# Products of a constant tile in TensorE's waits at five norms, in the pool layer and at the end of attention

## The chip, the cores and the metric

The kernel runs on one core of one Trainium2 chip. The metric is the device time of one execution in microseconds (us). The engines are TensorE (PE; its weight loads are shown as PEld), VectorE (DVE), ScalarE (ACT), GpSimd (POOL) and SyncE (SP), whose queue issues the weight transfers.
## What is computed

Two transformer blocks over 256 tokens of width 1024. The first block has one mixer made of three (an RWKV-7 recurrence, a sparse attention, an S5 state space), a convolutional FFN and a gated embedding ("ple"). The second block is two layers: a causal pooling mixer with an FFN, then dilated attention in three branches with an FFN. Cut to what matters here:

```
# first block, after its mixer
x = x + rms_norm(conv_ffn(rms_norm(x, pre_ffn_norm)), post_ffn_norm)   # FFN 0, norm 3 = post_ffn
x = x + rms_norm(p @ w_ple, ple_norm) * gate(x @ w_ple_gate)           # "pg" and "pl"
# second block
for layer in range(2):
    h = modulate(rmsnorm(x, norm1[layer]), sh1, sc1)      # norm 5 (layer 0), norm 7 (layer 1)
    if layer == 0: y = pool_mixer(h, w_in, w_grp, scale, w_out)
    else:
        kv = modulate(rmsnorm(x, kv_norm), ...) @ w_kv    # from the same x as norm 7
        y = dilated_attention(h, kv, w_q, w_o)
    x = x + g1 * y
    h = modulate(rmsnorm(x, norm2[layer]), sh2, sc2)      # norm 6 (layer 0), norm 8 (layer 1)
    x = x + g2 * conv_ffn(h, w_up, conv, w_down)          # FFN 1, FFN 2 (width 2816)
return rmsnorm(x, final_g)                                # norm 9
```

## The kernel before

Activations lie transposed: 8 tiles of 128 channels by 256 tokens. The program is written by hand, one instruction stream for each engine, with semaphores between them; TensorE executes its stream in order. Weights are streamed by SP as chunks of 1 MB into a ring of six slots. To reach the needed precision each fp32 operand is split in a high and a low part: ACT rounds a chunk to `ring_hi` (four slots), POOL subtracts it to give `ring_lo`, and TensorE does three products for each pair of tiles (high by high, high by low, low by high), accumulated in one of eight PSUM banks. A chunk gives two output tiles of 8 k-steps by 3 products, 48 products of 128x256.

Every dense stage follows an RMS norm of its input, and the norm is a chain that crosses the engines: TensorE sums the squares with `ones_mean` as one-column products (`mean_square_of`, called at the end of `ffn` and `last_tile`), ACT and DVE form the reciprocal root (`rs`), TensorE spreads it over a bank with four products by `ident` (`spread`, after it has waited on `rs_small`), DVE scales h by it, and ACT and DVE split the result, tile by tile, into `hn_hi` and `hn_lo`. TensorE begins the next stage in `first_tiles`: it opens three or four banks, waits for the chunks, and then for each k waits on `x_high` (the k-th high part is there) and does two products for each of the banks; the low parts come after, with `x_split`. The rest of the stage are `split_tile` calls, which wait for nothing but banks and chunks.

`opened(job)` takes the next bank in turn and waits until its last user is done; `held_back` and `gathered` take one out of the turn for a sum; `close` signals a finished job on `psum_ready`, in the order in which jobs were numbered.

The order of the work around the change is: `ple(3)`, `ffn(0, ...)` with norm 3 at its end, `projection(2, "pg", ...)` with norm 5 at its end (through `last_tile`), the pool layer (`first_tiles(3, ...)`, `grouped` and `pooled` by turns, the last of which is `pooled(3)` with its tiles 6 and 7), `projection(4, "po", ...)` with norm 6, `ffn(1, ...)` with norm 7, keys, values and attention, `dil_values(15)`, the output projection with norm 8, and `ffn(2, ...)` with norm 9. POOL writes the constants (`ident`, `ones_mean`, masks) at the start.

Of the kernel before, what the change touches and what calls it, by code (L numbers as in the profile page):

```python
# [10 lines left out]
F32 = mybir.dt.float32  # L11
# [5 lines left out]
P = 128  # L17
# [56 lines left out]
def two_block_kernel(nc, a, out):  # L74
    ctx = ExitStack()
    with ctx:
        sems = {}

        def sem(name):
            if name not in sems:  # L80
                sems[name] = ctx.enter_context(nc.semaphore(name))
            return sems[name]

        def sb(name, cols, rows=P):
            return ctx.enter_context(nc.sbuf_tensor(name, [rows, cols], F32))
# [4 lines left out]

        ident = sb("ident", P)
        ones_mean = sb("ones_mean", P)
        head_ones = sb("head_ones", P)
        head_mean = sb("head_mean", P)
# [369 lines left out]
        def _(pe):  # L465
# [29 lines left out]
            def opened(job):  # L495
                bank = next_bank()
                numbered(job, bank)
                return banks[:, bank, :]
# [23 lines left out]
            def chunk(key):  # L522

                if key not in begun:
                    in_turn(key)
                    begun.add(key)
                    if key == early[0]:
                        pe.wait_ge(sem("early_hi"), 1)
                    elif key in early:
                        pe.wait_ge(sem("early_lo"), early.index(key))  # L530
                    elif key in split:
                        pe.wait_ge(sem("lo_ready"), split_no[key] + 1)
                    else:
                        pe.wait_ge(*chunk_landed[key])
                used_at[key] = job_no[current[0]]
                chunk_used[key] = (psum_ready, used_at[key] + 1)
                if key in split or key in early:
                    k, n = KT if key in early else chunk_src[key][0].shape[1], 0
                    n = chunk_flat(key)[0].shape[1] // k
                    return [shaped(part, k, n) for part in chunk_flat(key)[1:]]  # L540
                return chunk_view(key)
# [8 lines left out]
            def close(ins, jobs=1):  # L550
                ins.then_inc(psum_ready, jobs)
# [44 lines left out]
                                            k == 0, k == KT - 1)  # L596
                close(last)

            def first_tiles(rnd, jobs, x, ks=tuple(range(KT)), ms=None, norm=None):

                low, high = x
                todo = []
                if norm is not None:
                    b_ms = opened(("ms", norm[0]))
                for job, key, c0 in jobs:
                    b = opened(job)[:, 0:T]
                    todo.append((b, [v[:, :, c0:c0 + P] for v in chunk(key)]))
                for n, k in enumerate(ks):
                    pe.wait_ge(sem("x_high"), KT * (rnd + 1) + n + 1)
                    for b, (w_lo, w_hi) in todo:  # L610
                        mm(b, w_hi[:, k, :], high[:, k, :], start=(n == 0), stop=False)
                        mm(b, w_lo[:, k, :], high[:, k, :], start=False, stop=False)
                for t, (b, (_, w_hi)) in enumerate(todo):
                    for n, k in enumerate(ks):
                        if t == 0:
                            pe.wait_ge(sem("x_split"), KT * (rnd + 1) + n + 1)
                        if t == 0 and n == KT - 1 and norm is not None:
                            mean_square_of(norm[0], b_ms, norm[1], (0,))
                        if t == len(todo) - 1 and n == KT - 1 and ms is not None:
                            gathered(ms)  # L620
                        last = mm(b, w_hi[:, k, :], low[:, k, :], start=False, stop=(n == KT - 1))
                    close(last, 2 if ms is not None and t == len(todo) - 1 else 1)

            def mean_square_of(i, b, sq, ks):

                for k in ks:
                    if i == 2:
                        pe.wait_ge(sem("squares_summed"), 1)
                    elif i in SUMMED and k == 0:
                        copied(("acc", i))  # L630
                    elif i in SUMMED:
                        pe.wait_ge(sem("squares"), square_base[i] + k + 1)
                    elif k % 2 == 0 or k == KT - 1:
                        pe.wait_ge(sem("squares"), square_base[i] + (1, 1, 2, 2, 3, 3, 4, 5)[k])
                    for s in range(2):
                        last = mm(b[:, s:s + 1], sq[:, k, s * P:s * P + P], ones_mean[:, 0:1],
                                  start=(k == s == 0), stop=(k == KT - 1 or i == 2), skip_group_check=True)
                if ks[-1] == KT - 1 or i == 2:
                    close(last)
                    if i in SUMMED:  # L640
                        held.remove(bank_no["acc", i])

            def spread(i, scratch=True):
                for x in range(3 if scratch else 0):
                    opened(("xs", i, x))
                b = opened(("wd", i))
                pe.wait_ge(sem("rs_small"), NORM_ORDER.index(i) + 1)
                for s in range(2):
                    last = mm(b[:, s * P:s * P + P], rs_of(i)[:, 2 + s:3 + s].broadcast_to([P, P]), ident[:, :])
                close(last, 4 if scratch else 1)  # L650

            def projection(rnd, name, key, x, ms=None, ks=tuple(range(KT))):

                tiles = [((name, m), (key, m // 2), 128 * (m % 2)) for m in range(8)]
                first_tiles(rnd, tiles[:4], x, ks, ms[0] if ms else None)
                for t in tiles[4:7]:
                    split_tile(*t, x)
                if ms is None:
                    split_tile(*tiles[7], x)
                    return  # L660
                last_tile(tiles[7][0], tiles[7][1], x, ms)

            def last_tile(job, key, x, ms):

                b = opened(job)
                current_job = current[0]
                b_ms = opened(("ms", ms[0]))
                current[0] = current_job
                w = chunk(key)
                for k in range(KT):  # L670
                    last = three_passes(b[:, 0:T], [v[:, k, 128:256] for v in w], [v[:, k, :] for v in x],
                                        k == 0, k == KT - 1)
                close(last)
                mean_square_of(ms[0], b_ms, ms[1], (0, 6, 7))
                if ms[0] != 1:
                    spread(ms[0])
# [488 lines left out]
            def ffn(f, first, ms):  # L1165
                tiles = [((nm, f, 2 * i + x), (nm, f, i), 128 * x) for i in range(FT // 2) for nm in ("ug", "uu")
                         for x in range(2)]
                begin = 4 if f else 3
                first_tiles(first, tiles[:begin], (hn_lo, hn_hi), norm=None if f else (2, sqb))
                if f == 0:  # L1170
                    for bank in kept:
                        held.remove(bank)
# [59 lines left out]
                            close(last_turn(s, k))  # L1232

            ple(3)
            ffn(0, 1, (3, sqb))
            projection(2, "pg", "pleg", (hn_lo, hn_hi), (5, sqb))

            def grouped(gq):
                for i in range(2):
# [7 lines left out]
                    close(last)  # L1247

            def pooled(gq):
                for s in range(2):  # L1250
                    copied(("pv", gq, s))
                for m in (2 * gq, 2 * gq + 1):
                    b = opened(("pp", m))
                    mm(b[:, 0:BAND0], pv[:, 0, m * P:m * P + P], bands[:, gq, 0:BAND0], stop=False, skip_group_check=True)
                    close(mm(b[:, P:T], pv[:, 1, m * P:m * P + P], bands[:, gq, BAND0:BAND0 + P], start=False,
                             skip_group_check=True))

            tiles = [(("pi", m), ("pin", m // 2), 128 * (m % 2)) for m in range(8)]
            first_tiles(3, tiles[:4], (hn_lo, hn_hi))
            split_tile(*tiles[4], (hn_lo, hn_hi))  # L1260
            pe.wait_ge(sem("bands_ready"), 1)
            grouped(0)
# [72 lines left out]
            def dil_values(i):  # L1335
# [18 lines left out]
                for x in range(2):  # L1354
# [2 lines left out]
                close(last)  # L1357

            first_tiles(6, [(("dk", 0, br, i), ("kv", 4 * br), 128 * i) for br in range(2) for i in range(2)],
                        (hn_lo, hn_hi))  # L1360
            for i in range(2):
                keys(0, 2, i)
            for br in range(3):
# [28 lines left out]
            for i in range(16):  # L1392
# [11 lines left out]
                if i >= 13:  # L1404
                    out_begun(2)
            dil_values(15)
            pe.wait_ge(sem("x_high"), KT * 10)
            pe.wait_ge(sem("x_split"), KT * 10)
            gathered(8)
            for m, bank in enumerate(out_banks):  # L1410
                numbered(("dw", m), bank)
                held.remove(bank)
# [66 lines left out]
        def _(pool):  # L1479
# [14 lines left out]
                keep_if(v, ALU.is_ge, size - 1, -1, neg)  # L1494

            led.emit(g.memset(ident[:, :], 0.0), sem("ident_ready"))
            keep_if(ident[:, :], ALU.not_equal, 0, 1, [[-1, P]], 1.0, sem("ident_ready"))
            led.emit(g.memset(ones_mean[:, :], 1.0 / D))
            led.emit(g.memset(head_ones[:, :], 1.0))
# [1469 lines left out]
```

## Time and profile before

| | |
|---|---|
| time, median of 3 runs | 1344.93 us (1342.05 to 1350.05) |
| span of the profiled execution | 1340.4 us |
| mean granted clock over the span | 0.974 |
| PEld, DVE, ACT, POOL busy | 89%, 42%, 46%, 63% |
| DMA | 242.82 MB, mean 181 GB/s |

The profiled execution is given by its span, from the first to the last instruction; no time of its own is given beside it. The runs' times are of other executions. The page has the busy time of each engine, the span in 40 slices, the chain of work that ended last, and the costliest groups of instructions. The granted clock of a stretch shows whether TensorE ran at its high level in it.

### The profile page before, as it was taken

What the parts mean: (1) busy time and instruction counts of PE and PEld (TensorE: products, weight loads), DVE (VectorE), ACT (ScalarE), POOL (GpSimd) and SP (SyncE); (2) the same over time, 40 slices, a digit from 0 to 9 for tenths busy, and PEclk for the clock granted to TensorE, in tenths of its full rate; (3) what the DMA queues carried; (4) which work ended last, traced back from release to release, by engine and by line L of the source; (5) the groups of instructions that cost most, each with busy time, mean ns of one, the idle gap of its engine ahead of it and who ended that gap; (6) DMA issues with size and microseconds to landing.
All of it is one profiled execution on the core that took longest, in us unless ns stands there. A gap on an engine that the chain in (4) does not pass through costs nothing.

```text
span 1340.4 us, 25785 instructions
## 1 busy us (share of the span) xinstructions
PE 1278.5 (95%) x10737; PEld 1192.8 (89%) x10737; DVE 564.4 (42%) x1275; ACT 621.8 (46%) x962; POOL 849.0 (63%) x441
## 2 busy tenths in 40 slices
PE   7998989889999999899999999999999998999998
PEld 6984548679999999899999999999998888999998
DVE  5658686633666653513333203132222224433301
ACT  5531443136655644653544434554534454544442
POOL 7985400027798696564887786856745665788772
PEclk9998999989999999898999999999999999999999
DMA  8749995504455555334555554453648793455550
GB/s 266 205 158 371 345 334 206 189 1 158 145 177 183 173 174 188 126 122 162 165 182 189 173 174 157 145 165 98 191 127 263 233 291 123 139 181 188 174 173 32
DMA packets 232817, 242.82 MB, mean 181 GB/s; under 512 B 9068, under 2 KB 201726, under 8 KB 232702
## 3 DMA queue, kind: packets, MB, share of 16 engines
q1 hardware_dynamic: 232382, 241.08, 55.3%
q8 instruction: 86, 1.41, 0.4%
q14 instruction: 29, 0.24, 0.1%
q10 hardware_dynamic: 320, 0.10, 0.0%
HBM read 240.11 MB, written 1.05 MB: 180 GB/s over the span
## 4 chain that ended last, share of the span: by engine, by line
PE 83%; DVE 4%; ACT 2%; issue 1%; DVEq 0%; ACTq 0%
PE banks L548 81%; PE banks L1332 1%; DVE arena L1693 1%; DVE arena L1686 1%; ACT arena L2432 1%; DVE banks L1686 0%; DVE banks L1693 0%; ACT ring_hi L2432 0%; DVE arena L1699 0%; ACT hn_hi L2432 0%; PE banks L558 0%; PE banks L861 0%; PE banks L984 0%; ACT L2432 0%; DVE arena L1690 0%
## 5 line engine op out<-in xcount | busy, mean ns | idle before, releaser
L1613 POOL TENSOR_TENSOR ring_lo<-ring,ring_hi 128x2048 fp32r<-128x2048 f32 (+1 forms) x176 | 719.0, 4096 | 423.5 <-ACT ring_hi L2432 423.4
L548 PE MATMUL banks<-hn_hi,ring_lo 128*128 128x256 f32 (+1 forms) x1864 | 525.4, 287 | 0.0
L548 PE MATMUL banks<-hn_hi,ring_hi 128*128 128x256 f32 x1696 | 484.0, 289 | 11.8 <-ACT hn_hi L2432 11.0
L548 PE MATMUL banks<-hn_lo,ring_hi 128*128 128x256 f32 x1696 | 445.8, 283 | 0.0
L2432 ACT ACTIVATE ring_hi<-ring 128x2048 fp32r<-128x2048 f32 (+1 forms) x176 | 299.6, 1704 | 171.2 <-PE banks L548 127.3
L548 PEld LDWEIGHTS banks<-hn_hi,ring_lo 128*128 128x128 f32 (+1 forms) x1864 | 363.6, 196 | 0.1
L548 PEld LDWEIGHTS banks<-hn_hi,ring_hi 128*128 128x128 f32 x1696 | 333.1, 196 | 15.2 <-issue 9.4
L548 PEld LDWEIGHTS banks<-hn_lo,ring_hi 128*128 128x128 f32 x1696 | 310.5, 192 | 0.1
L2432 ACT ACTIVATE arena<-banks 128x256 f32<-128x256 f32 (+6 forms) x238 | 92.4, 409 | 242.7 <-PE banks L548 173.0
L548 PEld LDWEIGHTS banks<-arena 64*128 64x128 f32 (+4 forms) x1282 | 115.4, 178 | 62.2 <-issue 38.9
L548 PE MATMUL banks<-arena 128*64 128x128 f32 (+9 forms) x1282 | 143.1, 305 | 21.2 <-DVE arena L1686 8.7
L548 PE MATMUL banks<-act_hi,ring_hi 128*128 128x256 f32 x528 | 149.7, 283 | 0.0
L548 PE MATMUL banks<-act_hi,ring_lo 128*128 128x256 f32 x528 | 149.4, 283 | 0.0
L548 PE MATMUL banks<-act_lo,ring_hi 128*128 128x256 f32 x528 | 149.4, 283 | 0.0
L1693 DVE SCALAR_TENSOR_TENSOR arena<-banks,par,arena 128x255 f32<-128x255 f32 (+1 forms) x187 | 89.6, 481 | 121.3 <-ACT arena L2432 118.8
L2432 ACT ACTIVATE arena<-banks,par 128x256 f32<-128x256 f32 x88 | 49.7, 565 | 123.0 <-PE banks L548 70.8
L548 PEld LDWEIGHTS banks<-act_lo,ring_hi 128*128 128x128 f32 x528 | 101.4, 192 | 0.0
L548 PEld LDWEIGHTS banks<-act_hi,ring_lo 128*128 128x128 f32 x528 | 101.4, 192 | 0.0
L548 PEld LDWEIGHTS banks<-act_hi,ring_hi 128*128 128x128 f32 x528 | 101.4, 192 | 0.0
L1693 DVE SCALAR_TENSOR_TENSOR h<-banks,mod,h 128x256 f32<-128x256 f32 x32 | 15.5, 484 | 134.8 <-PE banks L548 134.8
L2432 ACT ACTIVATE arena<-arena 128x256 f32<-128x256 f32 (+4 forms) x97 | 46.9, 512 | 36.5 <-DVE arena L1922 12.7
L548 PE MATMUL banks<-ring_lo,hn_hi 128*128 128x256 f32 x208 | 58.9, 283 | 0.0
(263 smaller groups left out, 1579.5 us busy)
## 6 DMA issues: line engine op xcount, KB each, us to landing
ring<-in_ada_w_dram SPq DMA_DIRECT2D x48, 1024.0 KB, 8.9
ring<-in_ffn_w_up_dram SPq DMA_DIRECT2D x44, 1024.0 KB, 5.2
ring<-in_w_up_dram SPq DMA_DIRECT2D x22, 1024.0 KB, 5.1
ring<-in_ffn_w_down_dram SPq DMA_DIRECT2D x16, 1024.0 KB, 4.9
ring<-in_w_kv_dram SPq DMA_DIRECT2D x15, 1024.0 KB, 5.5
ring<-in_w_in_dram SPq DMA_DIRECT2D x9, 1024.0 KB, 8.4
ring<-in_w_kv_dram SPq DMA_DIRECT2D x18, 512.0 KB, 4.0
ring<-in_attn_w_q_dram SPq DMA_DIRECT2D x18, 512.0 KB, 3.9
```

The costliest lines, as they stand in the source:

```text
L548: return nc.tensor.matmul(o, l, r, start=start, stop=stop, **k)
L1332: last = nc.tensor.transpose(b[:, br * P:br * P + P], dsc[s][:, x, k * P:k * P + P], ident[:, :])
L1613: led.emit(g.tensor_tensor(low, raw, high.bitcast(F32), ALU.subtract), sem("lo_ready"))
L1686: led.emit(v.tensor_tensor(o, x, y, op), signal, value)
L1693: led.emit(v.scalar_tensor_tensor(out=o, in0=x, scalar=s, in1=y, op0=op0, op1=op1), signal, value)
L2432: led.emit(nc.scalar.activation(o, x, func, **k), signal, value)
```

## The change

A constant tile `steady` of 128x128 ones (fp32r) is written by POOL at the start. A helper `steadied(o, n)` issues n products of it with itself, read as 256 columns, into a bank that the next job has opened and not yet begun; the job's first product starts the bank anew, so that what stood there is dropped. 112 such products are issued, each group ahead of one of TensorE's waits:

- in `spread`, 5 each at norms 3, 5, 6, 7 and 8, before the wait on `rs_small`;
- in `last_tile` at norm 5, 16 before the sums of squares;
- in `first_tiles` before the first wait on `x_high`: 13 at `projection(2, ...)`, 9 at the pool layer, 8 each at `ffn(1, ...)`, `ffn(2, ...)` and the keys;
- in `pooled`, 12 at tile 6; the bank is now opened before the wait for the copies (`copied(("pv", ...))`), in all four calls;
- after `dil_values(15)`, 13; `gathered(8)` is moved ahead of the waits on `x_high` and `x_split`.

TensorE's stream has in addition one wait on `steady_ready` after `ple(3)`.

```
+        steady = ctx.enter_context(nc.sbuf_tensor("steady", [P, P], F32R))
...
+            def steadied(o, n):
+                for _ in range(n):
+                    mm(o[:, 0:T], steady[:, :], steady[:, :].unsqueeze(1).broadcast_to([P, 2, P]))
...
-            def first_tiles(rnd, jobs, x, ks=tuple(range(KT)), ms=None, norm=None):
+            def first_tiles(rnd, jobs, x, ks=tuple(range(KT)), ms=None, norm=None, idle=0):
...
+                steadied(todo[0][0], idle)
                 for n, k in enumerate(ks):
                     pe.wait_ge(sem("x_high"), KT * (rnd + 1) + n + 1)
...
                 b = opened(("wd", i))
+                if i in (3, 5, 6, 7, 8):
+                    steadied(b, 5)
                 pe.wait_ge(sem("rs_small"), NORM_ORDER.index(i) + 1)
...
-            def projection(rnd, name, key, x, ms=None, ks=tuple(range(KT))):
+            def projection(rnd, name, key, x, ms=None, ks=tuple(range(KT)), idle=0):
...
-                first_tiles(rnd, tiles[:4], x, ks, ms[0] if ms else None)
+                first_tiles(rnd, tiles[:4], x, ks, ms[0] if ms else None, idle=idle)
...
                 close(last)
+                if ms[0] == 5:
+                    steadied(b_ms, 16)
                 mean_square_of(ms[0], b_ms, ms[1], (0, 6, 7))
...
-                first_tiles(first, tiles[:begin], (hn_lo, hn_hi), norm=None if f else (2, sqb))
+                first_tiles(first, tiles[:begin], (hn_lo, hn_hi), norm=None if f else (2, sqb), idle=8 if f else 0)
...
             ple(3)
+            pe.wait_ge(sem("steady_ready"), 1)
             ffn(0, 1, (3, sqb))
-            projection(2, "pg", "pleg", (hn_lo, hn_hi), (5, sqb))
+            projection(2, "pg", "pleg", (hn_lo, hn_hi), (5, sqb), idle=13)
...
             def pooled(gq):
-                for s in range(2):
-                    copied(("pv", gq, s))
                 for m in (2 * gq, 2 * gq + 1):
                     b = opened(("pp", m))
+                    if m == 6:
+                        steadied(b, 12)
+                    if m == 2 * gq:
+                        for s in range(2):
+                            copied(("pv", gq, s))
...
-            first_tiles(3, tiles[:4], (hn_lo, hn_hi))
+            first_tiles(3, tiles[:4], (hn_lo, hn_hi), idle=9)
...
-                        (hn_lo, hn_hi))
+                        (hn_lo, hn_hi), idle=8)
...
             dil_values(15)
+            gathered(8)
+            steadied(bank_of(("acc", 8)), 13)
             pe.wait_ge(sem("x_high"), KT * 10)
             pe.wait_ge(sem("x_split"), KT * 10)
-            gathered(8)
...
             led.emit(g.memset(ident[:, :], 0.0), sem("ident_ready"))
+            led.emit(g.memset(steady[:, :].bitcast(F32), 1.0), sem("steady_ready"))
```

## Rows read from the trace of the kernel before

**Rows 1.** The page: busy time, and the chain that ended last by engine.
```profile
PE 1278.5 (95%) x10737; PEld 1192.8 (89%) x10737; DVE 564.4 (42%) x1275; ACT 621.8 (46%) x962; POOL 849.0 (63%) x441
...
PE 83%; DVE 4%; ACT 2%; issue 1%; DVEq 0%; ACTq 0%
```

**Rows 2.** TensorE's waits by releaser: us in total, times, longest.
```profile
PE banks L548 <- ACT hn_hi L2432: 12.2, 13, 1.8
...
PE banks L548 <- DVE rs L1699: 4.1, 6, 0.8
```

**Rows 3.** Busy time by stretch; after the engines the granted clock, DMA share, GB/s.
```profile
530.46:537.29 6.83, 5.44 (x25) 5.47 (x26) 6.65 (x19) 3.72 (x12) 0.00 (x0) 0.50 0.22 75
561.18:568.01 6.83, 4.88 (x22) 4.58 (x22) 4.79 (x12) 3.09 (x9) 0.00 (x0) 0.50 0.10 30
602.14:605.55 3.41, 3.41 (x18) 3.41 (x18) 0.85 (x2) 1.17 (x4) 0.97 (x1) 0.50 1.10 360
629.45:636.28 6.83, 5.65 (x28) 5.55 (x27) 6.49 (x16) 3.95 (x9) 1.95 (x1) 0.50 0.26 87
827.42:830.83 3.41, 3.11 (x14) 3.14 (x15) 3.30 (x9) 2.09 (x6) 0.00 (x0) 0.50 0.15 50
1138.03:1144.86 6.83, 6.13 (x29) 6.16 (x30) 6.38 (x16) 4.56 (x9) 4.22 (x1) 0.50 0.25 79
```

**Rows 4.** TensorE in order of time around norm 3: start, us, instruction, idle before.
```profile
527.31 1.40 PE L548 MATMUL banks<-ones_mean,arena 128*128 128x1 f32 x12
529.35 0.68 PE L548 MATMUL banks<-ident,rs 128*128 128x128 f32 x4 [0.65 <-DVE rs L1699]
531.85 0.55 PE L548 MATMUL banks<-hn_hi,ring_hi 128*128 128x256 f32 x1 [1.81 <-ACT hn_hi L2432]
...
532.41 0.41 PE L548 MATMUL banks<-hn_hi,ring_hi 128*128 128x256 f32 x1
532.62 0.41 PE L548 MATMUL banks<-hn_hi,ring_lo 128*128 128x256 f32 x1
```

**Rows 5.** The chain that ended last, in order of time: FFN 1's products.
```profile
630.76 192.74 PE banks L548 x1584
```

**Rows 6.** ACT in order of time: last high parts after norms 3 and 6.
```profile
538.71 0.38 ACT L2432 ACTIVATE hn_hi<-banks 128x256 fp32r<-128x256 f32 x1
...
635.48 0.47 ACT L2432 ACTIVATE hn_hi<-banks,mod 128x256 fp32r<-128x256 f32 x1 [0.44 <-DVE banks L1693]
```

**Rows 7.** TensorE in order of time around norm 5.
```profile
559.74 1.50 PE L548 MATMUL banks<-ones_mean,arena 128*128 128x1 f32 x12 [2.24 <-DVE arena L1686]
562.01 1.19 PE L548 MATMUL banks<-ident,rs 128*128 128x128 f32 x4 [0.77 <-DVE rs L1699]
564.39 0.55 PE L548 MATMUL banks<-hn_hi,ring_hi 128*128 128x256 f32 x1 [1.18 <-ACT hn_hi L2432]
```

**Rows 8.** TensorE in order of time at the pool layer's last tiles.
```profile
600.83 1.17 PE L548 MATMUL banks<-late,arena 128*128 128x144 f32 x8 [1.88 <-ACT arena L2432]
```

**Rows 9.** TensorE in order of time around norm 7.
```profile
825.86 0.68 PE L548 MATMUL banks<-ident,rs 128*128 128x128 f32 x4 [0.74 <-DVE rs L1699]
827.72 0.55 PE L548 MATMUL banks<-hn_hi,ring_hi 128*128 128x256 f32 x1 [1.18 <-ACT hn_hi L2432]
```

**Rows 10.** TensorE in order of time at attention's end.
```profile
1124.06 0.36 PE L548 MATMUL banks<-hn_hi,ring_hi 128*128 128x256 f32 x1 [1.83 <-ACT hn_hi L2432]
```

**Rows 11.** Busy time by stretch: before norm 6's fall, and at attention's end.
```profile
626.03:629.45 3.42, 2.44 (x21) 2.23 (x19) 0.65 (x2) 0.68 (x2) 3.42 (x2) 1.00 0.45 137
...
1120.97:1124.38 3.41, 1.58 (x27) 1.36 (x24) 1.34 (x4) 1.00 (x2) 0.00 (x0) 1.00 0.01 2
```

**Rows 12.** POOL in order of time at the start.
```profile
1.46 0.20 POOL L1498 MEMSET ones_mean<- 128x128 f32 x1
...
12.25 4.55 POOL L1517 TENSOR_TENSOR ring_lo<-ring,early_hi 128x2048 fp32r<-128x2048 f32 x1 [0.45 <-ACT early_hi L2432]
```

**Rows 13.** The page's costliest group: POOL's low parts of the weights.
```profile
L1613 POOL TENSOR_TENSOR ring_lo<-ring,ring_hi 128x2048 fp32r<-128x2048 f32 (+1 forms) x176 | 719.0, 4096 | 423.5 <-ACT ring_hi L2432 423.4
```

## Prediction, made before the change was run

> **What bounds the kernel now.** I read the page first: TensorE is busy for 95% of the span and is 83% of the chain that ended last [rows 1]. A change gains only if TensorE's own work gets shorter or its waits do. Next its waits by releaser: the two steps of a norm that it waits for, the spread of the reciprocal root and the first high part, cost 4.1 and 12.2 us in all [rows 2]. The change shortens no such wait: what TensorE waits for is made by ACT and DVE. So I looked at the clock. In stretches around the norms the granted clock is 0.50, the 1.2 GHz level. Six of them lie at the places of the change, 34.1 us together: after norms 3, 5, 6, 7 and 8, and at the pool layer's end [rows 3]. Each begins inside or just after a wait, and for most of it TensorE has products to do; the order of time shows what they cost there: two products of 256 columns start 0.21 us apart (532.41, 532.62) [rows 4], and the same form runs at 192.74 / 1584 = 0.122 us in FFN 1, nearly all of it at 1.00 [rows 5]. That is what can be won: 0.213 less 0.122, or 43% of each slow stretch in which TensorE is bound by its own products. The 16 us of waits stay.
>
> **The change part by part.**
>
> *What the slow stretches cost.* At each place: the time from the first dense product to the end of the stretch, times 0.43.
> - Norm 3: 531.85 to 537.29 is 5.44 us, so 2.3 us. But here the high parts come slowly. The last begins at 538.71 and takes 0.38 [rows 6], and the products that wait for it would begin at about 539.2 and end at 540.2. As it is, 25 slow ones of the 64 are done by 537.29 and the other 39 end at 537.29 + 39 x 0.122 = 542.0. So the gain is 1.8 us.
> - Norm 5: 564.39 to 568.01 is 3.62 us, so 1.55. The four spreading products are slow too, 1.19 us [rows 7] for 0.68 at norm 7 [rows 9]: 0.5 more. Together 2.05.
> - Pool's end: the stretch of 3.41 us is full of products [rows 3]: 1.45.
> - Norm 6: 630.76 [rows 5] to 636.28 is 5.52 us: 2.35. The last high part is done at 635.95 [rows 6]; TensorE at full clock needs it at 630.76 + 56 x 0.122 = 637.6. It stays the bound, and the same holds for norms 5, 7 and 8, whose high parts follow the same steps.
> - Norm 7: 827.72 [rows 9] to 830.83 is 3.11 us: 1.35.
> - Norm 8: its wait is that of norm 7. The slow stretch has 6.13 us of TensorE's work in it, dense products [rows 3]: 2.6.
>
> The sum is 1.8 + 2.05 + 1.45 + 2.35 + 1.35 + 2.6 = 11.6 us.
>
> *Do the added products hold the clock?* No row before has a filler. What the rows show is which kind of work goes with a fall. Ahead of the fall at norm 6 TensorE is recorded busy for 2.44 of 3.42 us, and yet the clock falls [rows 11]; most of these records are one-column products such as those of rows 4, which last 0.12 us each and stream nothing. At attention's end the busy time is only 1.58 of 3.41 us, most of it wider products of attention's values, and the clock stays [rows 11]. So the recorded busy time alone does not tell; the kind of product matters, and the fillers are 256 columns wide. Bounds for the effect: 0 (they do nothing) and all of the 11.6. I take all of it, for the reason that they have the form of the stream in which the clock is 1.00.
> The Trainium skill, "TensorE: Matmul & The Clock Gate", Part 4 (PE-mode transpose), says that transposes do not count as busy for the gate in the way other products do. By that rule a kind that does not count would bring none of the 11.6; the fillers are plain products, but whether ones multiplied with ones count is what no row shows.
>
> *What the fillers cost.* One costs 0.122 us at the high level, 0.213 at the low one. They run in waits whose end ACT or DVE sets, so only what sticks out counts. Waits and fillers (at 0.122): norm 3, 0.65 for 5 (0.61) and 1.81 for 13 (1.59) [rows 4]; norm 5, 2.24 for 16 (1.95), 0.77 for 5 (0.61), 1.18 for 9 (1.10) [rows 7]; pool's end 1.88 for 12 (1.46) [rows 8]; norms 6, 7, 8 each 0.74 for 5 (0.61) and 1.18 for 8 (0.98) [rows 9], of which the other two are like it; attention's end 1.83 for 13 (1.59) [rows 10]. In all 112 fillers, 13.7 us, in 16.1 us of waits. Each fits, two with under 0.1 us to spare; I put 0.3 us for those, bounds 0 and 1. Behind the fillers on TensorE stand the spread and the first products, for which the whole next stage waits, so anything that sticks out is paid in full. At the low level the same 112 last 23.9 us, 7.8 more than the waits: that is the price if the cover is gone.
>
> *The moved steps.* In `pooled` the bank is opened before the wait for the copies; both waits were passed before the same product, so the later one still sets it: 0. The bank of tile 6 was last that of tile 3, long split. `gathered(8)` takes the bank of a transpose whose copies `dil_values(15)` had already waited for: 0. The wait on `steady_ready` is for something 500 us old.
>
> *The memset.* POOL gets one more 128x128 memset, 0.20 us by the one of the same size; POOL then waits 0.45 us for ACT before the first low part [rows 12]. Hidden; without that wait 0.2.
>
> *What is late next.* TensorE reaches each stage's later chunks up to 2.6 us sooner. POOL makes a chunk's low part in 4.1 us [rows 13], TensorE uses it up in 48 x 0.122 = 5.9 us, and during each norm the ring fills. So I expect no new wait for weights. If there were one at each stage, it could take back what was won: bounds 0 and 11.6, and I take 0.
>
> So this execution would be 11.6 - 0.3 = 11.3 us shorter: 1329.1 for its span of 1340.4. The median of the runs shown stands 4.5 us above that span; a time of the profiled execution itself is not given. All six places lost the clock in it, which an average execution need not do, and at two the stretch was half as long as elsewhere; I take 85% of the gain for the median: 9.6 us, **1335.3 us**. The Trainium skill, same page, Part 1, says that the number of slow products at a start changes from run to run of one kernel. That is no term of the sum; the rows of one execution can't show it.
>
> **The rivals.**
>
> *A. Ones do not count.* The clock falls as before and the fillers behind a fall run slow. For it: nothing in the trace shows such a product holding the clock. Against it: the form. Price by the starts of the slow stretches [rows 3]: at norm 3 the 13 fillers begin at 530.03, 4 run fast and 9 slow, 2.4 us in 1.81, 0.6 over; norm 5, 5 and 9 slow, 0.3 and 0.75 over; norm 6, 8 slow, 0.5 over; norm 8 0.15. Together 2.3: 1347.2 us.
>
> *B. The gain is won and given back.* The clock holds, but the next stage waits for weights or, as at norm 3, for the split of the activations. For it: at norm 3 the high parts are the bound as soon as the clock holds, and at the pool layer's end the DMA is at 360 GB/s in the slow stretch [rows 3]. Against it: POOL's 4.1 us a chunk. If half comes back, 11.3 / 2: about 5 us gained, 1340 us. A case that falls short of the whole for another cause, such as fewer falls in the runs, ends there too.
>
> *C. Slower: the fillers stick out.* One mechanism: they run at 0.213 us or more, because the clock is already low at each wait or each of them loads `steady` afresh without overlap. All 112 then cost 7.8 us over the waits and nothing is won: 1352.7 us. It is slower beyond what can be told only if a filler costs on average over (16.1 + 6.7) / 112 = 0.20 us, with no gain beside it. Against it: every product in the stream loads its own weights and takes 0.122.
>
> **How the numbers follow.** About 0.5%, 6.7 us, is what a measurement of this kernel can tell from no change. The forecast case gets 0.68, A 0.12, B 0.14, C 0.06. Of the forecast case (own range 1329 to 1339) a tenth gives under 6.7 us. Faster 0.62, same 0.32, slower 0.06. The range goes from 1329 (the whole 11.3 and a saving in variance between executions) to 1344, which takes in B and leaves most of A and C out.
>
> **What would show it.** Right: in the profile after, the six stretches of 0.50 are gone, the mean granted clock is about 0.99 (34.1 us at half are 0.013 of the span), the fillers last 0.12 us each, the first dense product of each stage starts at the same distance from the last sum of squares as before, and its successors are 0.12 apart. The stretches of 0.50 before 300 us and the one at the end stay. Wrong: a clock of 0.50 behind fillers (A), idle time before `ring_lo` or `hn_hi` products in the 10 us after a norm (B), or a spread that starts later after the squares than 0.74 us (C).

## The result and the profile after

The changed kernel takes 1337.23 us (median of 6 runs, 1330.9 to 1340.5), the kernel before 1346.61 us in as many (1342.05 to 1350.05). The ratio is 0.9924, 95% interval 0.9899 to 0.9949: 10.2 us less. The profiled execution has a span of 1329.0 us and a mean granted clock of 0.984; before it was 1340.4 and 0.974.

The page after, first busy time, then the chain. They are nearly those of [rows 1]: the busy time of TensorE has not gone down, since fillers took the place of slow products.

```profile
PE 1279.6 (96%) x10849; PEld 1194.0 (90%) x10849; DVE 564.3 (42%) x1275; ACT 621.1 (47%) x962; POOL 849.6 (64%) x442
...
PE 82%; DVE 4%; ACT 2%; issue 1%; POOL 1%; DMA 1%; DVEq 0%; ACTq 0%
```

Busy time by stretch, after, with the columns of [rows 3]: the 7 us behind norms 3, 6, 7, 8 and the pool layer, and the one slow stretch that is left of the 34.1 us, at norm 5. It is the second row, with 0.50.

```profile
528.72:535.55 6.83, 6.66 (x52) 6.09 (x51) 6.65 (x18) 3.29 (x10) 0.00 (x0) 1.00 0.28 98
559.92:563.33 3.41, 3.41 (x19) 3.41 (x18) 3.34 (x8) 2.06 (x5) 0.00 (x0) 0.50 0.00 0
...
597.00:604.00 7.00, 6.94 (x58) 6.97 (x59) 0.85 (x2) 1.75 (x5) 2.35 (x1) 1.00 0.85 285
624.30:631.10 6.80, 6.66 (x56) 6.46 (x55) 6.62 (x16) 4.09 (x9) 1.89 (x1) 1.00 0.22 74
818.70:825.50 6.80, 6.66 (x55) 6.46 (x55) 6.61 (x16) 4.08 (x9) 0.00 (x0) 1.00 0.23 78
1128.60:1135.40 6.80, 6.28 (x53) 6.31 (x53) 6.58 (x16) 4.05 (x9) 4.84 (x2) 1.00 0.30 97
```

The 52 products in the first row are not to be compared with the 25 of [rows 3] as they stand, since the fillers in front of the first dense product are among them. Counted from the first dense product of the stage, 25 dense products start in 5.44 us before (531.85 to 537.29) and 40 after (530.44 to 535.88).

TensorE in order of time after, around norm 3, 6 and 7: start, us, instruction, idle before. The fillers end about when the wait does, and the dense products, from the second on, start 0.12 us apart instead of 0.21.

```profile
526.99 0.47 PE L549 MATMUL banks<-ones_mean,arena 128*128 128x1 f32 x3
527.32 0.84 PE L549 MATMUL banks<-steady 128*128 128x256 f32 x5
528.01 0.71 PE L549 MATMUL banks<-ident,rs 128*128 128x128 f32 x4
528.48 1.79 PE L549 MATMUL banks<-steady 128*128 128x256 f32 x13
530.44 0.38 PE L549 MATMUL banks<-hn_hi,ring_hi 128*128 128x256 f32 x1 [0.17 <-ACT hn_hi L2449]
530.66 0.28 PE L549 MATMUL banks<-hn_hi,ring_lo 128*128 128x256 f32 x1
530.78 0.28 PE L549 MATMUL banks<-hn_hi,ring_hi 128*128 128x256 f32 x1
...
623.55 0.71 PE L549 MATMUL banks<-ident,rs 128*128 128x128 f32 x4
...
817.97 0.71 PE L549 MATMUL banks<-ident,rs 128*128 128x128 f32 x4
```

The same view around norm 5, where the clock fell at 559.92: the 9 fillers behind the spread run slowly and last 1.99 us, and with them the first dense products.

```profile
554.54 2.07 PE L549 MATMUL banks<-steady 128*128 128x256 f32 x16
556.94 1.50 PE L549 MATMUL banks<-ones_mean,arena 128*128 128x1 f32 x12 [0.33 <-DVE arena L1703]
558.30 0.84 PE L549 MATMUL banks<-steady 128*128 128x256 f32 x5
559.12 0.71 PE L549 MATMUL banks<-ident,rs 128*128 128x128 f32 x4
559.58 1.99 PE L549 MATMUL banks<-steady 128*128 128x256 f32 x9
561.37 0.42 PE L549 MATMUL banks<-hn_hi,ring_hi 128*128 128x256 f32 x1
561.59 0.41 PE L549 MATMUL banks<-hn_hi,ring_lo 128*128 128x256 f32 x1
```

And at norm 8: the 8 fillers of FFN 2 begin 0.52 us late, because they stand behind the wait for a weight chunk.

```profile
1127.89 0.71 PE L549 MATMUL banks<-ident,rs 128*128 128x128 f32 x4
1129.12 1.18 PE L549 MATMUL banks<-steady 128*128 128x256 f32 x8 [0.52 <-POOL ring_lo L1630]
1130.14 0.28 PE L549 MATMUL banks<-hn_hi,ring_hi 128*128 128x256 f32 x1
```

### The profile page after: what moved, and what is told of

The parts are those of the page before. It is cut to its first block, busy times and chain, and to the rows that moved or that the text cites. A ratio compares the mean times of both kernels' runs of the same rounds, so it can differ in the third digit from the quotient of the medians.

```text
span 1329.0 us, 26012 instructions
## 1 busy us (share of the span) xinstructions
PE 1279.6 (96%) x10849; PEld 1194.0 (90%) x10849; DVE 564.3 (42%) x1275; ACT 621.1 (47%) x962; POOL 849.6 (64%) x442
## 4 chain that ended last, share of the span: by engine, by line
PE 82%; DVE 4%; ACT 2%; issue 1%; POOL 1%; DMA 1%; DVEq 0%; ACTq 0%
PE banks L549 79%; PE banks L1347 1%; POOL ring_lo L1630 1%; DVE arena L1710 1%; DVE arena L1703 1%; ACT ring_hi L2449 1%; ACT arena L2449 1%; DMA ring<-in_w_kv_dram 1%; DVE banks L1703 0%; DVE arena L1716 0%; DVE banks L1710 0%; PE banks L559 0%; PE banks L872 0%; PE banks L995 0%; ACT hn_hi L2449 0%
## 5 line engine op out<-in xcount | busy, mean ns | idle before, releaser
L549 PE MATMUL banks<-hn_hi,ring_lo 128*128 128x256 f32 (+1 forms) x1864 | 517.6, 284 | 0.0
L549 PE MATMUL banks<-hn_hi,ring_hi 128*128 128x256 f32 x1696 | 476.1, 286 | 4.0 <-ACT hn_hi L2449 2.8
L549 PEld LDWEIGHTS banks<-hn_hi,ring_lo 128*128 128x128 f32 (+1 forms) x1864 | 356.8, 192 | 0.1
L549 PEld LDWEIGHTS banks<-hn_hi,ring_hi 128*128 128x128 f32 x1696 | 326.3, 192 | 7.8 <-ACT hn_hi L2449 4.4
```

Of the source, the lines that this page charges most:

```text
L549: return nc.tensor.matmul(o, l, r, start=start, stop=stop, **k)
```

## The experiments

Each was timed in five rounds against the kernel before, on the same chip, with 6 to 12 executions of its own. The ratio is that to before. "Slow from 500 us" is the sum of the stretches at 0.50 in the profiled execution from 500 us to the start of its last norm. "Slow in all" is worked out for each execution from its mean granted clock c and its span, (1 - c) x 2 x span, and averaged over the executions.

```
kernel             ratio   95% interval      slow from 500 us   slow in all   times from .. to
before                                        34.1               83.2          1341.8 .. 1350.8
the change         0.9924  0.9899 .. 0.9949    3.4               49.4          1330.9 .. 1340.5
e1_moves           1.0006  0.9984 .. 1.0028   34.1               82.1          1341.0 .. 1354.1
e2_narrow          1.0017  0.9998 .. 1.0035   34.1               87.1          1343.0 .. 1354.0
e3_zeros           0.9909  0.9880 .. 0.9939    6.8               48.9          1330.6 .. 1341.7
e4_double          0.9975  0.9955 .. 0.9996    0.0               54.2          1337.7 .. 1348.5
e5_transposes      0.9927  0.9902 .. 0.9952    3.4               49.2          1330.3 .. 1342.0
e6_early           0.9891  0.9866 .. 0.9915    0.0               27.9          1328.7 .. 1330.0
e7_half            0.9949  0.9926 .. 0.9973   10.2               58.4          1332.6 .. 1345.4
e8_no_first        0.9955  0.9932 .. 0.9977   13.7               58.8          1332.1 .. 1342.9
e9_early_only      0.9968  0.9950 .. 0.9986   34.1               60.1          1339.7 .. 1346.5
e10_behind_chunks  0.9882  0.9854 .. 0.9910    0.0               29.2          1330.0 .. 1333.4
```

The row of before is of the 29 executions that e1 to e4 were timed against. The 28 that e5 to e8 were timed against have 77.0 us slow in all, and the 17 of e9 and e10 have 82.3; so differences of a few us in that column say nothing.

**The moved steps without the products.**

```
             def steadied(o, n):
-                for _ in range(n):
-                    mm(o[:, 0:T], steady[:, :], ...)
+                return
```

> The change without its 112 products: the constant tile, its memset, the wait on it, the bank opened ahead of the copies in the pool layer and the sum's bank taken ahead of the waits at attention's end are all kept. Theory (the gain is the held clock): time as before, ratio 1.000 within its interval, and slow stretches (granted clock 0.50) at most or all of the six places, some 25 to 34 us of them from 500 us on. Rival (the moved steps or the shifted addresses bring the gain): the ratio stays at 0.992, about 10 us less than before.

Measured: 1.0006, all six stretches back. Busy time by stretch of this kernel, two of the six:

```profile
530.37:537.20 6.83, 5.40 (x25) 5.43 (x26) 6.65 (x19) 3.68 (x12) 0.00 (x0) 0.50 0.22 77
...
1137.94:1144.77 6.83, 5.88 (x27) 5.91 (x28) 6.63 (x16) 4.31 (x9) 4.48 (x1) 0.50 0.28 91
```

The moved steps, the memset and the shifted addresses do nothing that can be measured; the products bring the gain.

**The same number of products, 2 columns wide.**

```
-                    mm(o[:, 0:T], steady[:, :], steady[:, :].unsqueeze(1).broadcast_to([P, 2, P]))
+                    mm(o[:, 0:2], steady[:, :], steady[:, 0:2])
```

> The same 112 products at the same places, but each streams 2 columns where the change streams 256; the weight load of 128x128 is the same. Theory (what counts is the kind of product, and the gain is the held clock): the clock falls at most of the six places as before, and the ratio is 0.998 to 1.001. Rival 1 (keeping TensorE occupied or primed brings the gain, whatever it streams): ratio 0.992 to 0.994 and no fall. If each costs as much as a sum-of-squares product, 0.12 us, they fit in the waits like the wide ones.

Measured: 1.0017. TensorE in order of time at norm 3 of this kernel: the waits are nearly as full as with wide ones, 5 in 0.70 us and 13 in 1.59, and the dense products behind them are slow. Below it, busy time by stretch of the longest fall from 500 us on, at norm 5. (This execution has one of 23.9 us at 285 us besides, where no product was added, and is one of the slower ones of its kernel, so its time is not compared.)

```profile
537.47 0.70 PE L549 MATMUL banks<-steady 128*128 128x2 f32 x5
538.16 0.71 PE L549 MATMUL banks<-ident,rs 128*128 128x128 f32 x4
538.63 1.59 PE L549 MATMUL banks<-steady 128*128 128x2 f32 x13
540.59 0.58 PE L549 MATMUL banks<-hn_hi,ring_hi 128*128 128x256 f32 x1 [0.37 <-ACT hn_hi L2449]
540.97 0.42 PE L549 MATMUL banks<-hn_hi,ring_lo 128*128 128x256 f32 x1
```

```profile
567.88:578.12 10.24, 10.24 (x50) 10.24 (x50) 5.81 (x15) 4.85 (x10) 0.51 (x1) 0.50 0.20 67
```

So the gain does not come from keeping TensorE occupied or its weight loads going. It comes from the clock, and a narrow product does not hold it.

**Zeros in place of ones.**

```
-            led.emit(g.memset(steady[:, :].bitcast(F32), 1.0), sem("steady_ready"))
+            led.emit(g.memset(steady[:, :].bitcast(F32), 0.0), sem("steady_ready"))
```

> The change with zeros in the constant tile. Theory (the clock goes by what is streamed and not by its values): the same ratio as the change, 0.992, clock 1.00 behind five or six of the six waits. Rival (products whose values don't toggle anything don't count): the clock falls as before, the fillers behind a fall run at 0.213 us, and the time is 2 to 3 us over that of before, ratio 1.002.

Measured: 0.9909, the interval holds the change's ratio; slow time in all is 48.9 us against 49.4. The values do not matter here. This execution's profile shows that a fall can come back at a covered norm (568.32 and 1138.34, 3.4 us each), as in the change at norm 5.

**Twice as many.**

```
-                for _ in range(n):
+                for _ in range(2 * n):
```

> Twice as many products in every group, 224. Theory (what fits into a wait is free, what sticks out is paid in full because the next stage stands behind it): by the waits of the trace of before and 0.122 us each, 0.6 + 1.4 + 1.7 + 0.45 + 1.0 + 1.05 + 3 x (0.5 + 0.75) + 1.35 = 11.2 us over the waits. Against the change 9 to 11 us more, so about the time of before, ratio 0.998 to 1.001, at a clock held at all six places. Rival (TensorE's extra products are cheap wherever they stand, since another engine sets the time): ratio 0.992 as the change.

Measured: 0.9975, that is 0.0051 or 6.9 us over the change; the profiled spans, 1336.0 and 1329.0, differ by as much. No slow stretch is left from 500 us on. TensorE in order of time at norm 3:

```profile
528.14 1.43 PE L549 MATMUL banks<-steady 128*128 128x256 f32 x10
529.41 0.60 PE L549 MATMUL banks<-ident,rs 128*128 128x128 f32 x4
529.77 3.36 PE L549 MATMUL banks<-steady 128*128 128x256 f32 x26
532.97 0.28 PE L549 MATMUL banks<-hn_hi,ring_hi 128*128 128x256 f32 x1
```

From the spread to the first dense product it takes 3.56 us here and 2.43 in the change. What sticks out is paid, but less than the 11.2 us reckoned. A part of the difference is in the reckoning: "idle before" counts from the modelled end of the last product, and a filler starts 0.14 to 0.24 us ahead of that end (527.32 against 526.99 + 0.47, 528.48 against 528.01 + 0.71 in the change's rows). With an estimated 0.2 us in each of the 13 groups the sum is 8.6. Another part is that the change pays for its slow stretch at norm 5, which this version does not have. That the two make up the whole difference is not shown.

**Transposes.**

```
+                for _ in range((6 * n + 5) // 10):
+                    nc.tensor.transpose(o[:, 0:P], ident[:, :], ident[:, :])
```

> The fillers are 68 transposes of the identity (fp32, 128x128) in place of the 112 products, about the same time in each wait at the 0.15 to 0.2 us that four spreading products of that size took. Theory (any product that streams a good number of columns holds the clock): under 10 us of slow stretches from 500 us on, ratio 0.992 to 0.995. Rival (by the Trainium skill, TensorE: Matmul & The Clock Gate, Part 4, transposes don't count as busy in the same way): the clock falls at five or six places, over 25 us slow from 500 us on, ratio 0.999 to 1.003.

Measured: 0.9927, the same falls as the change (one, 3.4 us at norm 5). These 68 fp32 transposes hold the clock as well as the 112 products do, at five of the six places. That is against the rule of the Trainium skill (TensorE: Matmul & The Clock Gate, Part 4) weighed in the prediction, by which transposes do not count as busy in the same way; the page's figures are for bf16, and for this kind the measurement decides. TensorE in order of time at norm 3:

```profile
527.59 0.52 PE L603 MATMUL banks<-ident 128*128 128x128 f32 x3
528.28 0.71 PE L549 MATMUL banks<-ident,rs 128*128 128x128 f32 x4 [0.17 <-DVE rs L1716]
528.83 1.04 PE L603 MATMUL banks<-ident 128*128 128x128 f32 x8
530.71 0.38 PE L549 MATMUL banks<-hn_hi,ring_hi 128*128 128x256 f32 x1 [0.84 <-ACT hn_hi L2449]
530.94 0.28 PE L549 MATMUL banks<-hn_hi,ring_lo 128*128 128x256 f32 x1
```

They filled less of the wait (0.84 us idle are left) and held it all the same. The expectation had about the same time in each wait; that was too high.

**Half as many, and none in first_tiles.**

```
e7_half:      for _ in range(n // 2):
e8_no_first:  -                steadied(todo[0][0], idle)
```

> Half of the products in every group (2, 8, 6, 4, 6): 52. Theory: fewer hold the clock less surely; 5 to 15 us slow from 500 us on in the profile where the change has 3.4, ratio 0.993 to 0.996. Rival (half is enough, and the change's last products stick out of their waits and cost time): ratio 0.990 to 0.992.

> The change without the products ahead of the first wait on the high parts (13, 9, 8, 8, 8 in first_tiles); those of the spread, of the sums at norm 5, of the pool layer and of attention's end stay. Theory (each group keeps the clock only through its own wait, and the fall comes from the norm's whole chain of waits): the clock falls again at about half of the norms, 10 to 20 us slow from 500 us on, ratio 0.994 to 0.997. Rival (the products ahead of the spread are enough, the others only fill): as the change, 0.992.

Measured: 0.9949 and 0.9955, with 10.2 and 13.7 us slow from 500 us on and some 9 us more in all than the change. With fewer the clock falls again at some places, in the first at norms 5, 6 and 7 and in the second at 5 and 8, so both the number of products and the second group of a norm matter. The intervals overlap a little with the change's, so the times alone only suggest the direction; the slow time agrees.

**A version with the first block covered too.** The chain there has waits of up to 2.86 us at which the clock falls. This version adds 72 products in six of them to the change's 112, and puts those of `first_tiles` ahead of the waits for the weight chunks. The edit is condensed here to a line for each place.

```
+                b = opened(("np", i)); steadied(b, {10: 8, 11: 9}.get(i, 0)); pe.wait_ge(sem("nsa_probs"), i + 1)
+                b = opened(("nv", i)); steadied(b, 12 if i == 9 else 0); copied(("np", i))
+                b = opened(("cpv", s)); if s == 0: steadied(b, 20); copied(("vc",))
+                b = opened(("st", q)); steadied(b, {5: 12, 6: 7}.get(q, 0)); copied(("E", s, r))
+                b = opened(("gm", c)); if c == 0: steadied(b, 4); for s in range(2): copied(("ol", s))
+                # first_tiles: steadied on the first bank ahead of chunk(key)
```

> The change, and 72 more such products in six waits of the first block (20 before the compressed values, 12 and 8 and 9 in the last rounds of the sparse attention, 12 and 7 at the state products, 4 before the group means; each bank opened ahead of the wait), and the products of first_tiles put ahead of the wait for the weight chunks. Theory (slow clock in waits costs 0.3 us for each slow us, as over the runs so far): the falls near 113, 130, 191 and 280 us, 6.8 + 6.8 + 3.4 + 6.8 us in the changed kernel's profile, shrink by more than half; 4 to 6 us less than the change, ratio 0.986 to 0.989. Rival 1 (the first block is bound by ACT and DVE there, so TensorE's clock is worth nothing in it): falls gone, time as the change, 0.992. Rival 2 (opening the banks earlier or fillers that stick out delay that chain): 0.994 or more.

Measured: 1329.74 us, 0.9891, and the six executions lie within 1.2 us. It is faster than the kernel before. Against the change the intervals overlap a little (0.9866 to 0.9915 and 0.9899 to 0.9949); the slow time in all, 27.9 us against 49.4, and `e10_behind_chunks` below with 0.9882 point the same way. The ratio says 4.4 us less than the change, which is in the 4 to 6 expected. Busy time by stretch, first three of the change, then two of this version at the same steps:

```profile
129.85:136.68 6.83, 6.83 (x28) 3.12 (x28) 6.38 (x12) 1.26 (x5) 3.33 (x4) 0.50 0.38 122
191.29:194.70 3.41, 3.41 (x20) 0.83 (x18) 3.31 (x8) 0.60 (x1) 0.00 (x0) 0.50 0.34 132
280.03:286.86 6.83, 5.75 (x36) 5.14 (x36) 3.85 (x12) 0.00 (x0) 4.46 (x1) 0.50 0.01 2
```

```profile
127.00:134.00 7.00, 6.45 (x50) 5.02 (x52) 6.76 (x12) 0.39 (x1) 3.53 (x4) 1.00 1.00 367
...
279.00:286.00 7.00, 5.95 (x73) 5.23 (x67) 6.32 (x19) 2.29 (x2) 6.43 (x2) 1.00 0.01 2
```

Not all falls of the first block are gone. The one near 113 us stayed, and in this execution and that of `e10_behind_chunks` there is one at 175 us that the change's does not have. Busy time by stretch of this version:

```profile
113.89:120.72 6.83, 5.23 (x25) 2.05 (x24) 6.31 (x18) 0.86 (x5) 2.90 (x4) 0.50 1.06 390
...
175.33:182.16 6.83, 6.83 (x32) 3.52 (x30) 4.66 (x11) 5.80 (x13) 0.00 (x0) 0.50 0.63 231
```

**Which part of it.** `e9_early_only` takes the change's groups out of `e6_early`; `e10_behind_chunks` puts the products of `first_tiles` back behind the chunks.

> The 72 products of e6_early in the first block without the change's own 112; all moved steps are kept. Theory (the two sets work on different stretches and add): of the 1.1% that e6_early gains the change's part of 0.76 is missing, so ratio 0.995 to 0.998; the profile has 25 to 34 us of slow stretches from 500 us on, as before. And since the executions of e6_early lie within 1.2 us where those of the change spread over 10, the spread here should be narrow too, 2 to 5 us, if the first block's falls make it; if the spread stays at 8 to 10 us, it comes from the later falls. Rival (the first block is bound by ACT and DVE, and e6_early gained by its other edit, the products ahead of the chunk waits): ratio 0.999 to 1.001.

> e6_early with the products of first_tiles behind the wait for the weight chunks, where the change has them. Theory: only FFN 2 waits for a chunk there (0.52 us in the change's profile), so 0.3 to 0.5 us more than e6_early and nothing that the comparison can tell, ratio 0.989 to 0.990. Rival (this edit made e6_early's gain over the change): ratio 0.992, as the change.

Measured: 0.9968 for the first block alone, with all 34.1 us slow from 500 us on; 0.9882 for the other, the same as `e6_early` within the intervals. The gains of the two sets, 0.0076 and 0.0032, add to 0.0108; both together measured 0.0109. The order before or after the chunk is not measurable in the time, though the profiles show it: from norm 8's spread to the first dense product 2.27 us behind the chunks, 1.89 ahead of them. The narrow spread comes mostly with both sets: 6.8 us with the early ones alone (12 executions), 9.6 with the change alone, 1.2 and 3.4 with both (6 each). The expectation had asked for 2 to 5 or 8 to 10 us with the early ones alone, so it is not decided which of the falls make the spread.

## Why the prediction was right

The predicted 1335.3 us stand against 1337.2, the predicted gain of 9.6 us against 10.2 (6.9 to 13.6 by the interval). The median of before was 1.7 us higher in more runs. The mechanism is the forecast one; that the number is so close is in part luck, because two errors in the sum offset each other, as shown below.

*The clock as the source.* Shown: without the products all six stretches are back (e1), with narrow ones there is as much slow time (e2, 34.1 us, with a stretch at attention's end in place of the one at the pool layer's), and over all executions slow time is 49.4 us where it was 77.0 to 83.2. That is 28 to 34 us less, and by the profiles 30.7 of the 34.1 us of [rows 3] are gone.

*The terms.* Between the starts of the spreads in the two profiled executions (before from [rows 4, 7, 9] and the same rows at norms 6 and 8, 628.89 and 1136.87; after from the fences above and 559.12, 1127.89):

```
part                      before     after     gained   predicted
norm 3                    32.66      31.11      1.55     1.8
norm 5 and pool's end     66.88      64.43      2.45     2.05 + 1.45
norm 6                   196.97     194.42      2.55     2.35
norm 7, attention's end  311.01     309.92      1.09     1.35
norm 8 to the end        203.53     201.11      2.42     2.6
sum                                            10.06    11.6, less 0.3
```

Up to norm 3's spread another 1.34 us lie between the two executions, where the change adds nothing. Half of it, 0.67 us, is there by 89 us: of the first 16 dense products, from 12.6 us on, all run slow in the execution before (5.74 us) and 10 in the one after (6 in 0.96 us, 10 in 4.20). The fall at 90 us, which only the execution before has, comes on top, and part of what it costs is made up again before 127 us. So the span forecast for this execution, 1329.1 us, met the measured 1329.0 by luck: 10.06 us came from the places of the change and 1.34 from elsewhere. The term that was mis-sized is norm 5: I took the fall there to be gone, and it came back for 3.4 us in the profiled execution (and in those of e3, e5 and e7), with 9 slow fillers that stick out. The part shows 2.45 us for the 3.5 forecast. Between the fillers there lie the 12 one-column sum products, 1.50 us together; whether they bring the fall is not shown.

*Norm 3 limited by the high parts*: 1.55 us for 1.8, where full speed alone would have given 2.3. The limit is seen in DVE's 6.65 of 6.83 us behind the norm, and in the order of time. The 8 products of one high part start 0.12 us apart, about 0.95 us in all, but the groups of 8 start 1.18 us apart, as the high parts come. TensorE in order of time after, the first product of three such groups and the one ahead of the second:

```profile
533.63 0.38 PE L549 MATMUL banks<-hn_hi,ring_hi 128*128 128x256 f32 x1
...
534.57 0.28 PE L549 MATMUL banks<-hn_hi,ring_lo 128*128 128x256 f32 x1
534.81 0.39 PE L549 MATMUL banks<-hn_hi,ring_hi 128*128 128x256 f32 x1
...
535.99 0.38 PE L549 MATMUL banks<-hn_hi,ring_hi 128*128 128x256 f32 x1
```

*Fillers in waits cost nothing*: as forecast, and there was more room than reckoned (e4), except at norm 5, where they ran slow.

*No new wait for weights*: not quite. FFN 2's chunk was 0.52 us late, and because the fillers stand behind that wait, the first dense product came 2.25 us after the spread where it was 1.86; that is 0.4 us of rival B's mechanism.

*The 85%.* The factor was wrong in its reason, that an average execution need not lose the clock at all six places. The profiled executions of before, e1, e2 and e9, the ones without wide products or transposes there, all have 34.1 us slow from 500 us on, and the gain by the medians, 10.2 us, is that of the profiled pair at these places, 10.06. The factor stood in for the fall left at norm 5 and for the late chunk, which the prediction had not foreseen. That is luck.

*Rival A* fell with the profile after, where the clock is 1.00 behind the fillers at five of the six places; what it describes, slow fillers behind a fall, is seen at norm 5 alone. With e3 even zeros hold the clock. *Rival C*: 224 products cost 6.9 us over the change and are still not slower than before.

## What to carry to other kernels

Where a dense stage begins behind a chain over other engines, look at the granted clock behind the wait and not only at the wait. Fill the wait with wide products into a bank already opened and not yet begun, as many as fit by 0.12 us each, and put them ahead of every wait, that for the weights too (0.38 us less at norm 8 in the profiles, too little to tell in the time). Size the gain as 43% of the slow time in which TensorE is bound by its own products: the waits themselves stay. Then look in the profile for places where the clock falls all the same, as at norm 5 here.

## What the runs showed of the hardware

- Much of the scatter between executions goes with the clock. Over 74 executions of the kernel before, span and slow time in all go together with a correlation of 0.81, 0.27 us for each slow us. With both sets of fillers six executions lie within 1.2 and 3.4 us, where six of before lie within 8.0 and six of the change within 9.6.
- Recorded busy time of TensorE says little of whether the clock holds. In e2 the waits are nearly as full of records as in the change (0.37 us idle before the first dense product at norm 3, for 0.17) and the clock falls; with transposes that leave 0.84 us idle there (e5) it holds.
- Zeros and ones hold it alike (48.9 and 49.4 us slow in all). Whether dense random values would do so differently was not tried.
- The reason why norm 5 alone keeps a fall in four of the profiled executions is open. Fillers between its sum products were not tried.
